# Weight loads of 1 MB in place of 512 KB in a two-layer mLSTM and convolution trunk

## The reference

```
h = RMSNorm(x);  u = h @ W_in + b_in              # W_in: 2048 x 20496
q, k, v, o, z_a, gates, glu_a, glu_b, z_b, g_a, g_b = split(u)
A:  q, k = SiLU(depthwise conv, 5 taps);  bidirectional mLSTM, 4 heads of 512
    y_a = (RMSnorm_head(sigmoid(o) * mlstm(q, k, v, gates)) * w * SiLU(z_a)) @ W_A
B:  c = depthwise conv, 31 taps (glu_a * sigmoid(glu_b)) + b
    y_b = (SiLU(LayerNorm(c)) * SiLU(z_b)) @ W_B
x = x + (sigmoid(g_a) * y_a + sigmoid(g_b) * y_b) @ W_out
```

## Time and profile before

| | us |
|---|---|
| median of 3 runs (2414.7 to 2415.8) | 2415.79 |
| the profiled execution | 2415.88 |
| its span, first to last instruction | 2414.1 |
| PE busy | 2395.2 |
| VectorE (DVE) busy | 1955.1 |
| ScalarE (ACT) busy | 1390.3 |
| weight loads, each 512 KB | 832 |
| median from issue to landing, W_in | 3.7 |

### The profile page before, as it was taken

One profiled execution on the slowest core, in us unless ns is written; L12 is line 12 of the kernel. 1 busy time (PEld: TensorE's weight loads), 2 busy tenths in 40 slices (PEclk: granted clock), 3 DMA queues, 4 the chain that ended last, 5 costly groups with the idle time before them and its releaser, 6 DMA issues.

```text
span 2414.1 us, 38535 instructions
## 1 busy us (share of the span) xinstructions
PE 2395.2 (99%) x14014; PEld 2108.6 (87%) x14014; DVE 1955.1 (81%) x2941; ACT 1390.3 (58%) x1678; POOL 72.4 (3%) x46
## 2 busy tenths in 40 slices
PE   7999999999999999999999999999999999999998
PEld 6888888888888888888888888888888888888887
DVE  7888989899987886556678899999999887765565
ACT  5656464646465557555566655556555655665554
POOL 1000000000000000000000000000000000000000
PEclk9999999999999999999999999999999999999999
DMA  7666665656566666665656665666656666666654
GB/s 210 175 194 190 183 181 174 186 171 182 174 192 191 189 186 188 191 189 187 195 152 198 194 192 171 182 178 179 179 177 177 196 189 190 180 197 189 190 190 139
DMA packets 448175, 444.65 MB, mean 184 GB/s; under 512 B 18000, under 2 KB 445792, under 8 KB 448096
## 3 DMA queue, kind: packets, MB, share of 16 engines
q1 hardware_dynamic: 448096, 443.74, 61.8%
HBM read 441.59 MB, written 2.10 MB: 184 GB/s over the span
## 4 chain that ended last, share of the span: by engine, by line
PE 99%; DVE 0%; DMA 0%; ACT 0%; issue 0%; SPq 0%; ACTq 0%
PE ps L1484 58%; PE ps L1487 29%; PE ps L1502 5%; PE ps L1506 2%; PE px L1637 0%; PE px L1661 0%; PE px L1659 0%; PE px L1660 0%; PE px L1636 0%; PE px L1638 0%; PE ps L1705 0%; PE px L1589 0%; PE px L1645 0%; DMA M<-in_x_dram 0%; PE px L1557 0%; PE px L1542 0%
## 5 line engine op out<-in xcount | busy, mean ns | idle before, releaser
L1484 PE MATMUL ps<-Hs,W 128*128 128x512 f32 x4960 | 1543.6, 393 | 0.0
L793 DVE TENSOR_TENSOR W<-RAW,W 128x1024 fp32r<-128x1024 f32 x832 | 1022.5, 1236 | 378.9 <-ACT W L436 375.2
L436 ACT CAST W<-RAW 128x1024 fp32r<-128x1024 f32 x832 | 862.9, 1048 | 719.7 <-PE ps L1487 626.2
L1487 PEld LDWEIGHTS ps<-Hs,W 128*128 128x128 f32 x4960 | 931.4, 188 | 205.9
L1487 PE MATMUL ps<-Hs,W 128*128 128x256 f32 x4960 | 978.8, 279 | 0.0
L1484 PEld LDWEIGHTS ps<-Hs,W 128*128 128x128 f32 x4960 | 752.4, 188 | 1.9 <-issue 0.9
L944 DVE SCALAR_TENSOR_TENSOR ACC<-CP,CWT,ACC 128x256 f32<-128x256 f32 x928 | 387.5, 478 | 0.0
L1484 PE MATMUL ps<-YC,W 128*128 128x512 f32 x1152 | 359.2, 393 | 4.6 <-DVE W L793 3.5
L1487 PEld LDWEIGHTS ps<-YC,W 128*128 128x128 f32 x1152 | 217.2, 189 | 48.0
L1487 PE MATMUL ps<-YC,W 128*128 128x256 f32 x1152 | 228.0, 279 | 0.0
L1484 PEld LDWEIGHTS ps<-YC,W 128*128 128x128 f32 x1152 | 175.0, 188 | 5.3 <-DVE W L793 3.9
(11 more groups left out here) (227 smaller groups left out, 1137.1 us busy)
## 6 DMA issues: line engine op xcount, KB each, us to landing
RAW<-in_w_in_dram SPq DMA_DIRECT2D x640, 512.0 KB, 3.7
RAW<-in_w_a_dram SPq DMA_DIRECT2D x64, 512.0 KB, 3.4
RAW<-in_w_b_dram SPq DMA_DIRECT2D x64, 512.0 KB, 3.3
RAW<-in_w_out_dram SPq DMA_DIRECT2D x64, 512.0 KB, 4.3
M<-in_x_dram SPq DMA_DIRECT2D x2, 1024.0 KB, 7.6
HEAD<-in_b_in_dram SPq DMA_DIRECT2D x8, 256.0 KB, 4.5
out_dram<-M SPq DMA_DIRECT2D x4, 256.0 KB, 3.2
out_dram<-M SPq DMA_DIRECT2D x2, 512.0 KB, 4.8
```

The lines of the kernel that those rows point to most:

```text
L436: nc.scalar.copy(WH[:, c, :, :], RAW[:, c, :, :]).then_inc(hi_made, 1)
L793: v.tensor_tensor(WL[:, c, :, :], RAW[:, c, :, :], WH[:, c, :, :].bitcast(F32), ALU.subtract).then_inc(lo_made, 1)
L1484: mm(ps[:, 2 * q + t, :], WH[:, c, kk, t * P:t * P + P], act_in[:, kt, :], start=(kt == 0), stop=False)
L1487: i = mm(ps[:, 2 * q + t, S:2 * S], WL[:, c, kk, t * P:t * P + P], act_in[:, kt, 0:S], start=False, stop=(kt == KT - 1))
```

## The change

The four loads of the first pair stay as they are, under the name `load_first`, with semaphores of their own (`first_in`). All others are made by halves: one DMA of 1 MB fills places 0 and 1 of RAW, a second one places 2 and 3. Each waits until both of its places are free, and has one semaphore (`raw_in[0]`, `raw_in[1]`). ScalarE's casts of places 0 and 1 wait for the first, those of 2 and 3 for the second. The rings are as large as before, and nothing else is moved.

```diff
-        raw_in = [sem(f"raw_in{c}") for c in range(QC)]
+        first_in = [sem(f"first_in{c}") for c in range(QC)]
+        raw_in = [sem(f"raw_in{c}") for c in range(QC // 2)]
...
-            def load_quarter(w, l, col, n, c):
-
-                sp.wait_ge(lo_made, n * QC + (c + 1))
-                sp.dma_start(RAW[:, c, :, :], w[l, :, c * KQ:(c + 1) * KQ, ds(col, PC)]
-                             ).then_inc(raw_in[c], 16)
+            def load_first(c):
+
+                sp.wait_ge(lo_made, c + 1)
+                sp.dma_start(RAW[:, c, :, :], w_in_v[0, :, c * KQ:(c + 1) * KQ, ds(GLU_A, PC)]
+                             ).then_inc(first_in[c], 16)
 
             def load_pair(w, l, col, n):
 
-                for c in range(QC):
-                    load_quarter(w, l, col, n, c)
+                for half in range(QC // 2):
+                    c = 2 * half
+                    sp.wait_ge(lo_made, n * QC + (c + 2))
+                    sp.dma_start(RAW[:, c:c + 2, :, :].rearrange("p c k n -> p (c k) n"),
+                                 w[l, :, c * KQ:(c + 2) * KQ, ds(col, PC)]).then_inc(raw_in[half], 16)
...
-            def split_hi(n, c):
-
-                act.wait_ge(raw_in[c], n * 16 + 16)
+            def split_hi(n, c, first=False):
+
+                if first:
+                    act.wait_ge(first_in[c], 16)
+                else:
+                    act.wait_ge(raw_in[c // 2], n * 16)
                 act.wait_ge(multiplied, n * QC + (c + 1))
                 nc.scalar.copy(WH[:, c, :, :], RAW[:, c, :, :]).then_inc(hi_made, 1)
```

More of the change, by code:

```diff
@@ L311, in load_x @@
                              ).then_inc(x_rows_in[i], 16)
-            def load_quarter(w, l, col, n, c):
-                sp.wait_ge(lo_made, n * QC + (c + 1))
-                sp.dma_start(RAW[:, c, :, :], w[l, :, c * KQ:(c + 1) * KQ, ds(col, PC)]
-                             ).then_inc(raw_in[c], 16)
+            def load_first(c):
+                sp.wait_ge(lo_made, c + 1)
+                sp.dma_start(RAW[:, c, :, :], w_in_v[0, :, c * KQ:(c + 1) * KQ, ds(GLU_A, PC)]
+                             ).then_inc(first_in[c], 16)
             def load_pair(w, l, col, n):
-                for c in range(QC):
-                    load_quarter(w, l, col, n, c)
+                for half in range(QC // 2):
[3 more added lines that the diff above has]
+                                 w[l, :, c * KQ:(c + 2) * KQ, ds(col, PC)]).then_inc(raw_in[half], 16)
             load_x(0)
-            load_quarter(w_in_v, 0, GLU_A, 0, 0)
+            load_first(0)
             load_x(1)
             for c in range(1, QC):
-                load_quarter(w_in_v, 0, GLU_A, 0, c)
+                load_first(c)
             for dst, src in row_loads[1:]:
@@ L507, in _ @@
             weighed_high(0, 0, xw_first, 1)
-            split_hi(0, 0)
+            split_hi(0, 0, first=True)
             weighed_high(0, 1, xw_first, 2)
             weighed_high(0, 2, xw_first, 3)
-            split_hi(0, 1)
+            split_hi(0, 1, first=True)
             weighed_high(0, 3, xw_first, 4)
@@ L514, in _ @@
             square_rows(1)
-            split_hi(0, 2)
+            split_hi(0, 2, first=True)
             weighed_high(0, 5, xw_late, 1)
             weighed_high(0, 6, xw_first, 6)
-            split_hi(0, 3)
+            split_hi(0, 3, first=True)
             weighed_high(0, 7, xw_late, 2)
```

## The result

The changed kernel takes **2446.27 us** (median of 4 runs, 2443.46 to 2448.85) against 2415.80 for the kernel before (4 runs, 2414.70 to 2415.83): the ratio is 1.0126, with a 95% interval from 1.0114 to 1.0138. That is 30.5 us slower, where 17.5 were forecast, and outside the range (2419 to 2442). The profiled execution is the quickest of the four, 2443.46 us for a span of 2441.5 us, so what the trace accounts for is 27.4 us; the other three runs lost up to 5 us more. In this kernel every line from ScalarE's cast on stands seven lower: the cast is L443, the subtraction L800, the sum of high and low part L807, the big multiplications L1491 and L1494, the attention product L1666, and the issue of a half is L325.

The account below looks back on a forecast made before the run. PE (TensorE) was taken to bound the kernel, busy 2395.2 of 2414.1 us. Per layer 6.84 + 3 x 0.64 = 8.8 us, two layers 17.5, so 2415.9 + 17.5 = 2433.4 us; range 2419 to 2442.

Parts of the forecast that it names:

- What the change does to a load: Every load but the four first: a half starts later, lands as a whole, and takes 5.3 us from issue to cast.
- GLU stage, into head 0: From pair 5 to 17 the load loop sets the pace; VectorE 7.26 us late, 6.2 still late at head 0's attention product.
- A trip: GLU stage: load, cast, subtraction and the work up to the next freed place, 22.56 us; PE wants two pairs in 22.08.
- the reserve of 0.2 at the product: Each head: the last low part is ready 0.2 us before PE starts the attention product on it.
- In every head, pairs 5 to 8: Two late loads make VectorE 0.84 us late against 0.2 in reserve; heads 1 to 3 lose 0.64 us each.
- the second of the two loads: Each head: the half for places 0 and 1 of pair 7, with a lateness of 0.42 us.
- Where it is hidden: g_A, z_B, g_B and output stages, first half of each head and start of layer 0: cost put at 0.
- (1): GLU stage: the half lands in time; at a load of 4.6 us 1.8 per layer, 2419.5 us, not slower; chance 0.16.
- (2): Only the GLU stage pays, VectorE making up ground in head 0: 2.4 us per layer, 2420.7 us; chance 0.14.
- (3): Each half takes what two competing quarters would, 6.4 us: 31 us more, 2464 us; chance 0.06.
- (4): Larger transfers carry more and the time falls, at most to 2412.4 us; chance 0.02, shared with unseen fast causes.

Follow-up runs that it names:

- the runs with one and with both: Kernel before, still in quarters: couples issued only when the second place is free, 2415.33 us; even cast waiting for both quarters, 2416.26 us; both delays, 2449.14 us.
- the late start alone: Kernel before, quarters kept, but both of a couple issued only when the second place is free, each cast waiting for its own quarter: 2415.33 us for 2415.74.
- pair 6 alone: Kernel before with a half load only for places 0 and 1 of pair 6 of each head, 8 halves: 2419.90 us for 2415.72.
- fewer taps: Kernel before with halves in pairs 4 to 17 of each layer and one convolution tap in five left out of the GLU loop: 2421.04 us.

## Why the prediction was right and wrong, step by step

**"What the change does to a load": right.** 5.3 us from issue to cast was forecast; halves landed in 5.2 in the median. That a half has two delays, and that they bite together, the runs with one and with both bear out. The fit of the Trainium skill (page "DMA: Bandwidth & Descriptors", section on the anatomy of one DMA), made for another path of issue, gives an estimate of 4.4 us, 0.8 less than the halves took.

**"GLU stage, into head 0": right in mechanism, low by a tenth.** VectorE at pair 17 was to be 7.26 us late; over the stage it became 7.75 us later in layer 0 of the changed kernel (1.47 to 9.22) and 7.19 in layer 1. A trip costs 1.2 to 1.5 us more than before. The stage alone costs 13.4 us for two layers, where 12.0 were forecast (6.2 less 0.2). Of the 1.4 us, 0.3 is the reserve of 0.2 at the product, which was 0.03 in each layer; the rest is mostly the size of the trip. What I also missed is that the loads of places 2 and 3 cost 3.5 us when they alone are halves; here the larger loss covers them, which is luck.

**"In every head, pairs 5 to 8": wrong in size.** Two terms. The slip behind the second of the two loads was not 0.42 but 0.7 us, since GpSimd's add goes first; the forecast took the order of VectorE and GpSimd as fixed. (The first was 0.35 to 0.51, as forecast.) And the reserve of 0.2 us at the product was a difference of two clock readings, the end of one operation and the start of the next, which holds 0.05 of handover; the first matmul behind a wait costs 0.11 more. The reserve was 0.03. Heads 1 to 3: 1.0 to 1.3 us for 0.64. Together the heads cost 10.7 us where 5.1 were forecast. In head 0 of layer 0 another 1.2 us came from one load that landed after 6.38 us (VectorE slipped 1.63 us at pair 6); in layer 1 that load took 5.17. Why the one was slow I don't know.

**"Where it is hidden": half wrong, and the largest miss in kind.** The g_A, z_B, g_B and output stages hide it all, as forecast, and the rest of a head nearly all (10.7 us with all its halves, 9.4 with the two). For the start of layer 0 I put 0, and for that of layer 1 nothing at all, on the ground that "VectorE's next idle piece takes" the delay. The two starts cost 4.1 us. In layer 1, where the experiments show the path, VectorE was idle there because it waited for that very load's cast (1.92 us ahead of the subtraction at 1244.98); such idle time follows the load and takes nothing. That row was in the trace, and I didn't go from it to PE's gate matmuls, which stood at zero reserve behind it.

**The rivals.** (1), that it lands in time, and (2), that only the GLU stage pays, fell with the landing of 5.2 us and the heads' 10.7 us. (3) named 6.4 us for the load and 2464: the load is not so slow. That the time went 13 of the 31 us from my forecast to 2464 has other causes. (4), that larger transfers gain, fell: with the same waits, 1 MB and twice 512 KB take the same time within what these runs can tell, and the 192 halves of the last stages gained nothing. The Trainium skill's rule to batch to 1 MiB or more (page "DMA: Bandwidth & Descriptors") speaks of the share of peak bandwidth; here the queue took 58% of the DMA engines' time, and bandwidth was not what was short.

**The range** followed the load's time alone. It had no room for a term put at 0 or for a slip that doesn't follow the load. Starts and heads together make 14.8 us, for which the forecast had 5.1. The GLU stage's 1.4 us would have stayed inside it.

## What to carry to other kernels

A load in a ring has a round trip; making it larger lengthens the trip twice, by the later start and by the later whole. In this kernel only the two together bite. Look for the places where the consumer's release, the load, and the work on it follow each other without a gap, and count each of them against the old pace of that loop, not against the pace of the engine that bounds the kernel. Idle time ahead of an operation is cover only if something other than the delayed thing ends it: ask for the releaser of each idle piece before you put 0.

## What the runs showed of the hardware that I had not expected

- VectorE's subtraction of two operands and GpSimd's add exclude each other for whole instructions. Where the add went first, 1.21 us became 1.85 to 3.3, and the subtraction ended 1.08 or 1.09 us behind the add in all eight heads of each run looked at. Before, VectorE started 0.16 to 0.17 us ahead of the add in each head; an idle piece of 0.25 us was enough to change who goes first, and it cost 0.7 us whatever its length up to 1.7.
- Short waits of PE are dearer than their length, and not equally in every run: an idle piece of 0.86 us was followed by 3.4 us at half the clock in the traced run, and by the times in 3 of 10. That is the likely cause of the spread of the changed kernel's runs (5 us, for 1.1 before); their mean granted clocks run from 0.996 to 0.998, and the slowest two have the lowest. I didn't trace those runs, so this stays a likely cause. The gap of 1.2 us between the times of the kernel before (2414.7 and 2415.8) may have the same kind of cause: its profiled execution has 3.4 us at half the clock from 25.2 us on, while those of the runs with the late start alone, with pair 6 alone and with fewer taps have none there, and PE is 1.0 to 1.3 us ahead in them from pair 2 on. A difference of a microsecond between two single traces can come from that.
- Two quarters issued 0.4 us apart on one queue are served nearly in order: in the run with the late start alone they land 3.76 and 5.23 us after the first issue (medians over all couples), and the second lands when a half of the same bytes does, 5.2. A quarter by itself took 3.7.
